# Gate and up products with two moving halves side by side, and identity transposes queued ahead of TensorE's waits, in a two-block transformer kernel

## The chip, the cores and the metric

The kernel runs on one core of a Trainium2 chip. The metric is the time of one execution on the device in microseconds (us), the median of several. TensorE multiplies matrices and writes to eight banks of PSUM, VectorE and ScalarE do the elementwise work, GpSimd takes some of it, and SyncE issues most DMAs. A bank holds 512 float32 values in each of 128 partitions.

## The reference

Two blocks follow each other, all in float32. The change touches the feed-forward layers of the first block, the norm ahead of the feed-forward in both layers of the second block, the very first norm, and the start of the attentions of the first block.

```python
D_MODEL, SEQ, FFN_HIDDEN = 1024, 256, 2816

def rms_norm(x, g):
    return x * rsqrt(mean(x * x, -1) + EPS) * g

def swiglu(h, w_gate, w_up, w_down):
    return (silu(h @ w_gate) * (h @ w_up)) @ w_down

# first block, for each of 2 layers: x is (256, 1024)
x = x + mixer(rms_norm(x, mix_norm))
x = x + memory_cross_attention(rms_norm(x, x_norm), rms_norm(mem, mem_norm), ...)
x = x + swiglu(rms_norm(x, ffn_norm), w_gate, w_up, w_down)

# second block, for each of 2 layers: h is (256, 1024), hc is (256, 1024)
h = h + g1 * mix                     # mix from a modulated norm of h
h = h + g2 * sq_relu_mlp(modulate(rms_norm_2(h, norm2_g), sh2, sc2), w_ff1, w_ff2)
# in layer 0 the same for hc; its 256 tokens stand beside those of h
```

## The kernel before

**Split products.** A float32 product is made of three. Each operand x is held as a high part (rounded to the format fp32r) and a low part (x minus the high part), and a product is high*high + high*low + low*high. Activations lie as [feature, token], eight tiles of 128 features (`KD` = 8) by `S` = 256 tokens. Weights come from memory as pieces of 512 KB, four of which fit in `RAW`. Two pieces make one unit: 1024 rows by 256 columns of a weight matrix. ScalarE rounds a piece to its high part (L1473), VectorE subtracts it from the raw values (L2024, which also frees the piece in `RAW` for the next DMA). Two split units fit (`NSPLIT` = 2), so unit s is split once TensorE has finished with unit s-2, and TensorE waits for the last L2024 of a unit before it starts on it. Below, "the split" of a unit is these four instructions, two on each engine.

**Two ways to order a unit on TensorE.** `project` (L787) keeps one bank for both 128-column halves of a unit and for each half and feature tile issues three matmuls of 256 columns: weights high by activations high (L696), high by low (L697), low by high (L698). `side_by_side` (L722) gives each 128-column half a bank of its own. Its left half collects high*high plus low*high, its right half high*low, so that one matmul of 512 columns takes the activations' high and low parts side by side (L746, the first one L742), and one of 256 columns the low weights (L745, L743). The two halves of the bank have to be added afterwards: ScalarE or VectorE copies or adds the one, VectorE adds the other. Before, the down products of the first block and the feed-forward of layer 1 of the second block use `side_by_side`; the gate and up products use `project`. In layer 1 of the second block ScalarE copies the right half of a bank (L1926), and VectorE adds the left half to it (L2700).

**The four accumulators.** `bank()` hands out PSUM banks `acc0` to `acc3` in turn; TensorE waits until the bank of four groups ago has been read. `pst`, `pso` and `pss` are banks for other uses.

**The feed-forward of the first block.** Its 2816 hidden features go in three chunks of 8, 8 and 6 tiles. A chunk is made in pairs of units, gate and up, four pairs, four and three: 22 units in a layer, 44 in all. The norm's factor for each token is applied to the products: VectorE multiplies the gate bank by it (L2177), ScalarE takes the SiLU (L1810), VectorE multiplies by the factor again (L2544) and by the up bank (L2548), ScalarE rounds the result (L1569), VectorE takes the low part (L2047). The first gate unit is followed by the sums of squares for the norm, and the factor is known only after the first up unit, when `spread` (L882) has copied it to all partitions. Between these stand the splits of later units, in an order written out by hand. In layer 0 GpSimd issues 16 DMAs of 476 KB (`skew`), one for each second split.

**Norms.** `mean_square` (L872) sums squares over the partitions with a matrix of ones, ScalarE takes the root (L1553), VectorE inverts it (L2073), `spread` (L882) copies it to all partitions, and VectorE (L2100, L2145, L2047, L2050) and ScalarE (L1569, L1582) make the normed tiles, one after the other. The product behind a norm takes the feature tiles as they come (`arriving`, L711 to L713, or `side_by_side` with `ready`).

**Attentions.** `attention` (L908) issues for a pair of heads the scores (L921), the transposes of the probabilities (L933) and the sums over values (L948), one pair ahead of the other engines' softmax. The first block has in layer 0 an attention of 16 heads, in layer 1 one of 16, and in each a cross attention of four.

## Time and profile before

| | us |
|---|---|
| median of 3 runs | 2003.89 |
| lowest, highest | 2003.71, 2009.75 |
| the profiled execution, its own time | 2004.48 |
| its span, first to last instruction | 2002.6 |
| TensorE busy | 1940.7 (97%) |
| VectorE, ScalarE busy | 1261.5, 885.9 |

Times in the profile count from the start of the span. The profile lists for each stretch the clock that TensorE was granted: 1.00 is 2.4 GHz and 0.50 is 1.2 GHz. A matmul's own duration includes the time until its result is written, and the next one starts earlier than that, so what a stream of matmuls costs is read from the distance of their starts. The mean granted clock over the span is 0.994.

### The profile page before, as it was taken

The numbers are of one execution on the slowest core, as the hardware profiler recorded it, in microseconds if no ns is written. First come the engines' busy times: TensorE is split into PE (matmuls) and PEld (weight loads), VectorE is DVE, ScalarE is ACT, GpSimd is POOL, SyncE is SP. The second block draws the span as 40 slices with busy tenths as digits, with TensorE's granted clock in tenths as the row PEclk, the third lists the DMA queues.
The fourth block names the chain that finished last, engine by engine and source line by source line (L and its number), as shares of the span: only waits on it lengthen the run. The fifth ranks groups of instructions, "written<-read, shape, count | busy, mean of one in ns | idle before, by whom it ended". The sixth has DMA issues, their size and how long they took to land.

```text
span 2002.6 us, 33109 instructions
## 1 busy us (share of the span) xinstructions
PE 1940.7 (97%) x13572; PEld 1703.3 (85%) x13572; DVE 1261.5 (63%) x2184; ACT 885.9 (44%) x1508; POOL 167.0 (8%) x187
## 2 busy tenths in 40 slices
PE   7999999999999999999999999999999999999998
PEld 7769999998689999978688887888888998997887
DVE  6765666677556666544434447667677745677776
ACT  5655543445565444424532334322232536455443
POOL 0220000002103100002511000000000012000000
PEclk9999999999999999999999999999999999999999
DMA  7365699955646565323533333454656422664554
GB/s 239 102 214 165 157 234 220 220 171 165 224 145 189 182 214 161 116 77 125 163 96 100 95 106 110 133 179 155 197 180 198 139 85 62 186 195 140 182 183 137
DMA packets 313325, 317.56 MB, mean 159 GB/s; under 512 B 17079, under 2 KB 291398, under 8 KB 312918
## 3 DMA queue, kind: packets, MB, share of 16 engines
q1 hardware_dynamic: 308156, 301.65, 49.6%
q0 software_dynamic: 3904, 12.03, 3.0%
q8 instruction: 108, 1.77, 0.4%
q10 hardware_dynamic: 1114, 1.76, 0.3%
q14 instruction: 43, 0.35, 0.1%
HBM read 306.54 MB, written 8.85 MB: 157 GB/s over the span
## 4 chain that ended last, share of the span: by engine, by line
PE 86%; DVE 7%; ACT 3%; DMA 2%; issue 1%; POOL 0%; SPq 0%; DVEq 0%; ACTq 0%; POOLq 0%
PE acc L696 20%; PE acc L697 19%; PE acc L698 19%; PE acc L746 8%; PE acc L745 4%; DVE w_low L2024 3%; PE pss L921 2%; PE acc L742 1%; PE acc L711 1%; ACT w_high L1473 1%; PE pst L933 1%; PE acc L712 1%; PE acc L713 1%; DMA raw<-in_w_mod 1%; PE acc L948 1%
## 5 line engine op out<-in xcount | busy, mean ns | idle before, releaser
L2024 DVE TENSOR_TENSOR w_low<-raw,w_high 128x1024 fp32r<-128x1024 f32 (+4 forms) x503 | 561.1, 1156 | 140.5 <-ACT w_high L1473 137.3
L1473 ACT ACTIVATE w_high<-raw 128x1024 fp32r<-128x1024 f32 (+4 forms) x503 | 471.7, 984 | 375.6 <-PE acc L698 234.2
L696 PE MATMUL acc<-normed,w_high 128*128 128x256 f32 (+1 forms) x1768 | 565.6, 320 | 0.7 <-DVE w_low L2024 0.6
L698 PE MATMUL acc<-normed,w_low 128*128 128x256 f32 (+1 forms) x1768 | 560.6, 317 | 0.0
L697 PE MATMUL acc<-normed,w_high 128*128 128x256 f32 (+1 forms) x1768 | 560.6, 317 | 0.0
L696 PEld LDWEIGHTS acc<-normed,w_high 128*128 128x128 f32 x1768 | 336.1, 190 | 27.0 <-issue 2.0
L698 PEld LDWEIGHTS acc<-normed,w_low 128*128 128x128 f32 x1768 | 336.2, 190 | 22.5
L697 PEld LDWEIGHTS acc<-normed,w_high 128*128 128x128 f32 x1768 | 336.3, 190 | 22.0
L746 PE MATMUL acc<-inner,w_high 128*128 128x512 f32 x612 | 218.2, 396 | 0.0
L696 PE MATMUL acc<-inner,w_high 128*128 128x512 f32 (+2 forms) x576 | 197.3, 343 | 2.2 <-DVE w_low L2024 2.0
L697 PE MATMUL acc<-inner,w_high 128*128 128x512 f32 (+2 forms) x576 | 196.0, 340 | 0.0
L698 PE MATMUL acc<-inner,w_low 128*128 128x512 f32 (+2 forms) x576 | 195.9, 340 | 0.0
L745 PE MATMUL acc<-inner,w_low 128*128 128x256 f32 x612 | 170.7, 279 | 0.0
L746 PEld LDWEIGHTS acc<-inner,w_high 128*128 128x128 f32 x612 | 114.9, 188 | 23.4
L696 PEld LDWEIGHTS acc<-inner,w_high 128*128 128x128 f32 (+1 forms) x576 | 108.4, 188 | 16.6 <-DVE w_low L2024 2.4
L745 PEld LDWEIGHTS acc<-inner,w_low 128*128 128x128 f32 x612 | 115.3, 188 | 4.2
L698 PEld LDWEIGHTS acc<-inner,w_low 128*128 128x128 f32 (+1 forms) x576 | 108.4, 188 | 12.2
L697 PEld LDWEIGHTS acc<-inner,w_high 128*128 128x128 f32 (+1 forms) x576 | 108.5, 188 | 12.1
L1569 ACT ACTIVATE inner<-probs_t 128x512 fp32r<-128x512 f32 x79 | 49.6, 629 | 140.0 <-DVE probs_t L2548 82.0
L696 PE MATMUL acc<-w_high,normed 128*128 128x256 f32 (+1 forms) x336 | 96.9, 289 | 0.6 <-ACT resid L1490 0.6
L697 PE MATMUL acc<-w_low,normed 128*128 128x256 f32 (+1 forms) x336 | 94.9, 282 | 0.0
L698 PE MATMUL acc<-w_high,normed 128*128 128x256 f32 (+1 forms) x336 | 94.9, 282 | 0.0
(281 smaller groups left out, 2685.9 us busy)
## 6 DMA issues: line engine op xcount, KB each, us to landing
raw<-in_w_ff SPq DMA_DIRECT2D x128, 512.0 KB, 4.2
raw<-in_w_mod SPq DMA_DIRECT2D x96, 512.0 KB, 4.4
raw<-in_w_in SPq DMA_DIRECT2D x84, 512.0 KB, 4.1
raw<-in_l_w_gate SPq DMA_DIRECT2D x44, 512.0 KB, 5.5
raw<-in_l_w_up SPq DMA_DIRECT2D x44, 512.0 KB, 4.5
raw<-in_l_w_down SPq DMA_DIRECT2D x32, 512.0 KB, 4.5
raw<-in_l_w_qkv SPq DMA_DIRECT2D x24, 512.0 KB, 4.6
raw<-in_l_w_out SPq DMA_DIRECT2D x16, 512.0 KB, 4.4
```

What stands on the lines that cost most here:

```text
L696: mm(dst, lh, rh, start=i == 0, stop=False)
L697: mm(dst, lh, rl, start=False, stop=False)
L698: ins = mm(dst, ll, rh, start=False, stop=i == n - 1)
L711: mm(dst, lh, rh, start=k == 0 and j == 0, stop=False)
L712: mm(dst, lh, rl, start=False, stop=False)
L713: ins = mm(dst, ll, rh, start=False, stop=k == kt - 1 and j == len(outs) - 1)
L745: mm(b[:, 0:S], wl[:, k, c], high, start=False, stop=False)
L746: ins = mm(out, wh[:, k, c], two, start=False, stop=k == kt - 1)
L921: ins = mm(PSS[e][:, at:at + k.shape[1]], q, k, start=True, stop=True)
L1473: nc.scalar.activation(WH[:, s % NSPLIT, w0:w0 + nw], RAW[:, r:r + nw], ACT.Copy).then_inc(w_high, 1)
L1569: nc.scalar.activation(d.high, tmp_like(i, d.high), ACT.Copy).then_inc(high_done, 1)
L2024: V.tensor_tensor(WL[:, s % NSPLIT, c], RAW[:, r:r + nw], WH[:, s % NSPLIT, c].bitcast(F32), ALU.subtract).then_inc(w_low, 1)
```

## The change

It has four parts.

1. Gate and up products go by `side_by_side`. What `project` put in one bank for a unit now lies in two, in halves to be added. New helpers do that, `second_halves` on ScalarE (into `SM` for the gate, into `TMP` for up) and `first_halves` on VectorE. The multiplication by the norm's factor reads SBUF now.
2. ScalarE and VectorE take the split behind an up unit ahead of rounding the pair's result (`highs`, `flush`); before, it came behind.
3. Three norms get transposes of the identity matrix into a bank that is unused at the time (`keep_busy`): 6 before the input has arrived, 8 ahead of `spread` and 14 behind it in the first norm; in the feed-forward norms of the second block 5 ahead of the last two tiles' squares, 12 and 24 around `spread` in layer 0, 8 and 14 in layer 1.
4. The attentions get them as well: 9 and 7 at the first of layer 0, 5 and 6 at the first of layer 1, 15 at each cross attention.

```diff
+            def keep_busy(n, spare):
+                for _ in range(n):
+                    nc.tensor.transpose(spare[:, 0:P], ident, ident)
...
-            def mean_square(sq, nt, T):
+            def mean_square(sq, nt, T, busy=0):
                 for k in range(nt):
+                    if k == nt - 2:
+                        keep_busy(busy, PSO)
...
                 for j in range(pairs + 2):
+                    keep_busy(busy.get((j, "turn"), 0), PSACC[st["acc"] % 4])
                     if 0 < j <= pairs:
                         turn(2 * j - 2)
                     if j + 1 < pairs:
+                        keep_busy(busy.get((j, "scores"), 0), PSO)
...
+                    keep_busy(busy.get((j, "second"), 0), PSO)
                     if 0 < j <= pairs:
                         turn(2 * j - 1)
...
+            keep_busy(6, PSO)
             pe.wait_ge(x_in, 16)
...
             mean_square(sq_x, KD, S)
+            keep_busy(8, PSO)
             spread(S)
+            keep_busy(14, PSO)
...
-                attention(x_tasks, ...)
+                attention(x_tasks, ..., busy={(2, "turn"): 15})
...
-                        project(1, at_pair, ready=ready)
+                        side_by_side(1, at_pair, ready=ready)
                         mean_square(sq1, KD, S)
-                        project(1, at_pair)
+                        side_by_side(1, at_pair)
                         spread(S)
-                        project(tiles - 2, at_pair)
+                        side_by_side(tiles - 2, at_pair)
...
-                mean_square(sq2 if T == 2 * S else sq1, KD, T)
+                mean_square(sq2 if T == 2 * S else sq1, KD, T, busy=5)
+                keep_busy(12 if T == 2 * S else 8, PSO)
                 spread(T)
+                keep_busy(24 if T == 2 * S else 14, PSO)
...
+            def second_halves(dst):                        # ScalarE
+                for j in range(2):
+                    b, free = bank()
+                    nc.scalar.activation(dst[:, S * j:S * j + S], b[:, S:2 * S], ACT.Copy).then_inc(relu_done, 1)
...
+            def first_halves(dst):                         # VectorE
+                for j in range(2):
+                    b, free = bank()
+                    st["relu"] += 1
+                    dve.wait_ge(relu_done, st["relu"])
+                    half = dst[:, S * j:S * j + S]
+                    V.tensor_tensor(half, half, b[:, 0:S], ALU.add).then_inc(free, 1)
+                    own(free)
```

**TensorE, one tile of a gate unit.** In the rows of an order, `acc<-normed,w_high` is the output bank and what is read, and the sizes are columns of the output. Before:

```order
L696 MATMUL acc<-normed,w_high 128x256
L697 MATMUL acc<-normed,w_high 128x256
L698 MATMUL acc<-normed,w_low 128x256
L696 MATMUL acc<-normed,w_high 128x256
L697 MATMUL acc<-normed,w_high 128x256
```

and after (L746 and L747 are the lines L745 and L746 of before):

```order
L747 MATMUL acc<-normed,w_high 128x512
L746 MATMUL acc<-normed,w_low 128x256
L747 MATMUL acc<-normed,w_high 128x512
L746 MATMUL acc<-normed,w_low 128x256
```

Three matmuls of 256 columns have become one of 512 and one of 256.

**VectorE, one pair in the middle of a chunk.** `scores` is the tile `SM`, `probs_t` the tile `TMP`, `inner` the pair's result. Before:

```order
L2177 SCALAR_TENSOR_TENSOR scores<-acc,scores 128x512
L2024 TENSOR_TENSOR w_low<-raw,w_high 128x1024 x2
L2544 TENSOR_TENSOR scores<-scores 128x512
L2548 TENSOR_TENSOR probs_t<-scores,acc 128x512
L2047 TENSOR_TENSOR inner<-probs_t,inner 128x512
```

and after:

```order
L2319 TENSOR_TENSOR scores<-scores,acc 128x256 x2
L2570 TENSOR_TENSOR scores<-scores 128x512
L2043 TENSOR_TENSOR w_low<-raw,w_high 128x1024 x2
L2573 TENSOR_TENSOR scores<-scores 128x512
L2319 TENSOR_TENSOR probs_t<-probs_t,acc 128x256 x2
L2578 TENSOR_TENSOR probs_t<-scores,probs_t 128x512
L2043 TENSOR_TENSOR w_low<-raw,w_high 128x1024 x2
```

Four additions are new, and the second split (the last row) has moved ahead of the low part of the result, which follows it.

**TensorE, the feed-forward norm of layer 0 in the second block.** `work` holds the squares, `cst` the constants. Before:

```order
L872 MATMUL acc1<-work,cst 32x128 x32
L882 MATMUL pst<-rstd,cst 128x128 x4
L711 MATMUL acc2<-normed,w_high 128x512
L712 MATMUL acc2<-normed,w_high 128x512
L713 MATMUL acc2<-normed,w_low 128x512
```

and after:

```order
L875 MATMUL acc1<-work,cst 32x128 x24
L897 MATMUL pso<-cst 128x128 x5
L875 MATMUL acc1<-work,cst 32x128 x8
L897 MATMUL pso<-cst 128x128 x12
L885 MATMUL pst<-rstd,cst 128x128 x4
L897 MATMUL pso<-cst 128x128 x24
L712 MATMUL acc2<-normed,w_high 128x512
```

41 transposes (L897) stand in the queue ahead of the waits for the last squares, for the inverse root and for the first normed tile.

## Rows read from the trace of the kernel before

**Rows 1.** The page: which engine holds the chain that ended last.
```profile
PE 86%; DVE 7%; ACT 3%; DMA 2%; issue 1%; POOL 0%; SPq 0%; DVEq 0%; ACTq 0%; POOLq 0%
```

**Rows 2.** TensorE in four stretches: stretch, length, busy (records), clock, DMA share, GB/s.
```profile
628.20:708.87 80.67, 80.67 (x674) 1.00 0.59 181
232.94:314.30 81.36, 81.13 (x675) 1.00 0.95 223
708.87:731.25 22.38, 22.38 (x130) 1.00 0.66 201
1878.28:1901.50 23.22, 22.83 (x130) 1.00 0.52 163
```

**Rows 3.** TensorE in a down unit, in order of time: start, duration, line, operands.
```profile
710.32 0.28 PE L745 MATMUL acc<-inner,w_low 128*128 128x256 f32 x1
710.44 0.40 PE L746 MATMUL acc<-inner,w_high 128*128 128x512 f32 x1
710.67 0.28 PE L745 MATMUL acc<-inner,w_low 128*128 128x256 f32 x1
```

**Rows 4.** Groups by line, 636 to 706 and 1878.2 to 1901.4: count, busy, mean ns, idle before.
```profile
L1473 ACT ACTIVATE w_high<-raw 128x1024 fp32r<-128x1024 f32 x25 | 25.0, 1047 | 14.7 <-PE acc L698 14.7
...
L2024 DVE TENSOR_TENSOR w_low<-raw,w_high 128x1024 fp32r<-128x1024 f32 x26 | 30.7, 1222 | 4.1 <-ACT w_high L1473 4.1
...
L2700 DVE TENSOR_TENSOR scores<-scores,acc 128x256 f32<-128x256 f32 x7 | 2.9, 417 | 2.5 <-ACT scores L1926 2.4
...
L1926 ACT ACTIVATE scores<-acc 128x256 f32<-128x256 f32 x8 | 3.0, 376 | 6.9 <-PE acc L746 6.9
```

**Rows 5.** Weight pieces, from issue to landing, in 243 to 314 (layer 0), then 636 to 706 (layer 1).
```profile
DMA to landing us min/median/max: 3.6/7.3/10.6
...
DMA to landing us min/median/max: 3.5/4.4/5.5
```

**Rows 6.** VectorE in order of time in the first pair of layer 0.
```profile
237.25 1.23 DVE L2024 TENSOR_TENSOR w_low<-raw,w_high 128x1024 fp32r<-128x1024 f32 x1 [1.80 <-ACT w_high L1473]
239.20 0.69 DVE L2544 TENSOR_TENSOR scores<-scores 128x512 f32<-128x512 f32 x1 [0.72 <-ACT scores L1810]
```

**Rows 7.** Half-clock stretches: length, busy of PE, PEld, DVE, ACT, POOL, then clock.
```profile
17.00:20.30 3.30, 3.28 (x15) 2.84 (x14) 3.23 (x8) 1.65 (x3) 0.00 (x0) 0.50 1.05 415
...
597.30:600.60 3.30, 3.05 (x10) 2.09 (x8) 1.72 (x2) 0.22 (x1) 0.00 (x0) 0.50 0.44 105
...
1208.30:1211.60 3.30, 3.30 (x9) 2.55 (x9) 3.23 (x9) 1.82 (x4) 0.00 (x0) 0.50 0.00 0
...
1805.60:1812.30 6.70, 6.05 (x18) 4.89 (x19) 6.41 (x15) 3.09 (x7) 0.00 (x0) 0.50 0.01 2
```

**Rows 8.** TensorE's transposes of the inputs, first at the start, then at 24 us.
```profile
6.26 3.65 PE L1075 MATMUL acc<-cst,work 128*128 128x128 f32 x16 [6.26 <-DMA work<-in_x]
...
24.01 1.91 PE L1075 MATMUL acc<-cst,work 128*128 128x128 f32 x16
```

**Rows 9.** TensorE in the cross attention and at its output product, layer 0, then layer 1.
```profile
201.61 0.63 PE L933 MATMUL pst<-cst,scores 128*128 128x128 f32 x4 [2.02 <-DVE scores L2380]
...
207.42 0.47 PE L711 MATMUL acc<-inner,w_high 128*128 128x256 f32 x1
...
595.39 0.63 PE L933 MATMUL pst<-cst,scores 128*128 128x128 f32 x4 [2.02 <-DVE scores L2380]
...
602.68 0.47 PE L711 MATMUL acc<-inner,w_high 128*128 128x256 f32 x1
```

**Rows 10.** The chain of waits behind the feed-forward norm of layer 0, second block.
```profile
1218.91 2.28 DVE w_low L2024 x2
1221.24 0.50 PE acc L696
```

**Rows 11.** Layer 1: TensorE's L742 (ns min/median/max, first and last start), VectorE's split.
```profile
L742 PE MATMUL acc<-normed,w_high x3: 398/628/765, 1806.2 to 1814.9; 128*128 128x512 f32 x3
...
1811.78 2.35 DVE L2024 TENSOR_TENSOR w_low<-raw,w_high 128x1024 fp32r<-128x1024 f32 x2
```

More of the change, by code:

```diff
@@ L558, in build @@
         gated = sem("gated")
+        gate_scaled = sem("gate_scaled")
         rot_done = sem("rot_done")
@@ L906, in rotate, with attention @@
                     ins.then_inc(acc_full, 1)
-            def attention(tasks, mods=0, lead=None, tail=None, keys=None, ropes=None, late=None):
+            def attention(tasks, mods=0, lead=None, tail=None, keys=None, ropes=None, late=None, busy={}):
                 first, pairs = st["task"], len(tasks) // 2
@@ L1159, in _ @@
                     attention(swa_tasks + mla_tasks, MODS, lead=mla_lead, tail=heads_product, late=SWA_H // 2,
-                              keys=st["acc"] - 3)
+                              keys=st["acc"] - 3, busy={(1, "scores"): 9, (2, "turn"): 7})
                 else:
@@ L1175, in _ @@
                     values(1)
-                    attention(dil_tasks, MODS, lead=lambda: values(1), tail=heads_product)
+                    attention(dil_tasks, MODS, lead=lambda: values(1), tail=heads_product, busy={(1, "scores"): 5, (1, "second"): 6})
                 pe.wait_ge(cols_free, st["pair"])
@@ L1184, in _ @@
                 project(2, at_pair, ready=by_tile(S))
-                attention(x_tasks, lead=lambda: values(1, blocks=(2, 3)), keys=st["acc"] - 2)
+                attention(x_tasks, lead=lambda: values(1, blocks=(2, 3)), keys=st["acc"] - 2, busy={(2, "turn"): 15})
                 project(2, ot, m=4, kt=4, ready=by_head_tile(4))
@@ L1923, in _ @@
                             if l:
-                                for j in range(2):
-                                    b, free = bank()
-                                    nc.scalar.activation(SM[:, st["sig"] % 2, S * j:S * j + S], b[:, S:2 * S],
-                                                         ACT.Copy).then_inc(relu_done, 1)
+                                second_halves(SM[:, st["sig"] % 2, :])
                                 st["sig"] += 1
@@ L2540, in _ @@
                                 rooted_row()
-                            times_row(gate, g)
+                            V.tensor_tensor(gate, gate, RROW2, ALU.mult).then_inc(gate_scaled, 1)
                             split()
@@ L2544, in _ @@
                             link(V.tensor_tensor(gate, gate, RROW2, ALU.mult))
-                            b, free = bank()
                             i = room()
                             d = hidden(c, S).tiles(m, m + 2)
-                            V.tensor_tensor(TMP[:, i % 2, :].rearrange("p (a n) -> p a n", a=2), gate,
-                                            b[:].rearrange("p (a n) -> p a n", a=2), ALU.mult).then_inc(free, 1)
+                            up = TMP[:, i % 2, :]
+                            first_halves(up)
+                            V.tensor_tensor(up, raw_gate, up, ALU.mult).then_inc(val_done, 1)
                             pending.append((i, d, None))
-                            flush()
                             if m or c:
                                 split()
+                            flush()
                     else:
@@ L2694, in _ @@
                                 st["sig"] += 1
-                                for j in range(2):
-                                    b, free = bank()
-                                    st["relu"] += 1
-                                    dve.wait_ge(relu_done, st["relu"])
-                                    half = s[:, S * j:S * j + S]
-                                    V.tensor_tensor(half, half, b[:, 0:S], ALU.add).then_inc(free, 1)
-                                    own(free)
+                                first_halves(s)
                                 V.scalar_tensor_tensor(TMP[:, i % 2, :], s, 0.0, s, ALU.max, ALU.mult)\
```

22 lines of the change are left out of this document (11 added, 11 removed).

## The prediction

> **What bounds the kernel now.** First I read who holds the chain that ended last: TensorE for 86% of it, VectorE 7% [rows 1]. So an edit counts by what it does to the distance between TensorE's matmuls and to its waits. Then I read windows. Fourteen gate and up units take 80.67 us in layer 1 of the first block with no idle time, so a unit costs 80.67/14 = 5.762 us, and its 48 matmuls of 256 columns 0.120 us each. In layer 0 the same fourteen take 81.36 us, 5.811 each: 0.7 us more, at a DMA share of 0.95 against 0.59 [rows 2]. Third, the four places at half the clock that the change aims at [rows 7].
>
> **Part 1, the products.** Four down units, already in the new form, take 22.38 us, 5.595 each, with nothing idle [rows 2]. There the 256 columns cost 710.44 - 710.32 = 0.12 us and the 512 columns 710.67 - 710.44 = 0.23 [rows 3], where three of 256 cost 0.36. A unit saves 5.762 - 5.595 = 0.167 us. There are 44, 22 in each layer: **7.4 us** if TensorE stays the bound, 3.7 in each layer.
>
> The Trainium skill, page "TensorE: Matmul & The Clock Gate", section "Back-to-back issue gap", gives a single warm matmul as its columns divided by 2.4 GHz plus 2.5 ns, which makes the merger worth 2.5 ns. By that the 704 mergers would save 1.8 us. The rows above show about 10 ns for each, and they decide.
>
> What is added is on the other engines. For each pair ScalarE gets four copies of 0.376 us and VectorE four additions of 0.417 [rows 4]. VectorE then has in a pair of 2 x 5.595 = 11.19 us: four L2024 of 1.222 = 4.9, four additions = 1.7, four operations of 512 columns of 0.69 (L2544's duration [rows 6]) = 2.8, together 9.3. ScalarE has four L1473 of 1.047, four copies and two more operations, of 0.7 at most each, about 7.1 [rows 4]. Neither is the bound, so what matters is the order. After a gate unit ends come one copy 0.38, two additions 0.83, the factor 0.69, the split's two L2024 2.44: 4.3 us, and TensorE needs that split 5.6 us after. After the up unit: 0.38 + 0.83 + 0.69 (product) + 2.44 = 4.3, again of 5.6. So the slack is 1.3 us, thanks to part 2, which puts the split ahead of the pair's result. The low part of the result (0.69) comes after, at 5.0, before the next gate unit ends at 5.6. What hides the copies and additions is thus 1.3 us; each us beyond it in a unit is paid in full.
>
> Every product now waits in two banks of the ring of four. In the middle of a chunk the banks come free as said, 1.2 us after their unit ends, and are wanted at 5.6: no wait. The first pair of layer 0 is the exception. VectorE's L2024 for the second piece of a late unit runs from 237.25 to 238.48, and it multiplies by the factor (L2544) at 239.20 to 239.89 [rows 6]. The new addition for the first up unit stands behind that and frees its first bank at 239.9 + 0.4 = 240.3. The second up unit wants that bank when the second gate unit ends: 232.94 [rows 2] less 0.3 (two faster units) plus 5.6 = 238.2. A new wait of **2.1 us**, bounded by 0 (if the pieces land earlier) and 3.5 (if the factor and the SiLU slip as far again as an L2024). In layer 1 I expect none: the DMA share is 0.59.
>
> The DMAs: four pieces fit, each is wanted once in a pair, and a landing plus L1473 and L2024 (1.05 + 1.22) has to fit in 11.2 us: it may take 8.9, before it was 11.5 - 2.3 = 9.2. In layer 1 landings take 4.4 us median, 5.5 at most: no matter. In layer 0 the median is 7.3, the longest 10.6 [rows 5]: some are over either bound, and TensorE's 0.7 us of waits there come from them. Each late one now costs up to 0.3 more. With all eleven pairs that is 3.7, with none it is 0, and the wait in the first pair may even absorb the 0.7 of before. I take **0.4**, near the low end, since the median is under the bound.
>
> Products: 3.7 + 3.7 - 2.1 - 0.4 = **4.9 us**, between 0 and 8.1.
>
> **Parts 3 and 4, the transposes.** A transpose costs 0.109 us at the full clock ((1.91 - 0.27)/15 between starts) and 0.215 at half ((3.65 - 0.42)/15) [rows 8]. TensorE did nothing but such transposes from 6.26 us on, and the full clock was there at 10.1, so transposes raise it. Whether five to fifteen of them also keep it from falling, no row shows: bounds nothing and all.
>
> The same page, section "Part 4: PE-mode transpose", says that "HAM K=8/8 doesn't engage for transpose-mode", which would make this half of the change worth nothing. The start of this trace speaks against it; the time that it would give is rival B.
>
> The queues ahead of the attentions' waits: 15 at the cross attention are 1.64 us in a wait of 2.02 and what follows it [rows 9]; those at the heads (9, 7, 5, 6) are 0.98 us at most in waits of like length. I charge nothing for them; if a wait is shorter than its transposes, the rest is paid, 0.3 us at most each. In order of time:
>
> - The six before the input land in idle time, but the last may overrun: -0.1.
> - 16.95 to 20.36, first norm: half the clock under 3.28 us of busy TensorE, so at most 1.6. But the tiles that it multiplies come from VectorE, busy for 3.23 of the 3.30 us [rows 7]; were it alone the bound, the gain would be 0. I take 0.6, nearer to that.
> - 597.2 to 600.6, the cross attention of layer 1. From the first transposes to the output product layer 0 takes 207.42 - 201.61 = 5.81 us, layer 1 602.68 - 595.39 = 7.29 [rows 9], and the latter holds a stretch at half the clock [rows 7]. At the full clock 7.29 becomes 5.81: +1.5, the best founded of them. In layer 0 there is nothing to gain.
> - 1208.2 to 1211.6, the norm of layer 0 in the second block. VectorE makes the tiles, again busy for 3.23 of 3.30 us [rows 7], and the unit behind waits for VectorE's L2024, 1218.91 + 2.28, TensorE starting at 1221.24 [rows 10]: what TensorE gains before that it waits there. No gain. Five transposes ahead of the last squares (0.55 us) partly delay the chain: -0.3.
> - 1805.5 to 1812.4, layer 1. Half the clock costs 6.05/2 = 3.0 us of work [rows 7], but the unit behind needs the low weights, ready at 1811.78 + 2.35 = 1814.1, and starts at 1814.9 [rows 11]. It can come no earlier than 1814.1: +0.8.
>
> Transposes: -0.1 + 0.6 + 1.5 - 0.3 + 0.8 = **2.5 us**, between -0.7 (none works, each place overruns) and 4.5.
>
> **The sum.** 4.9 + 2.5 = 7.4 us. The profiled execution took 2004.48, so it would take 1997.1; the median is 0.6 lower, so I predict **1996.5 us**.
>
> **Rivals.**
>
> A, the forecast: 1996.5. Chance 0.45.
>
> B, transposes do not hold the clock. For: nowhere in the trace does a short run of them stand in a wait. Against: the clock at 10.1 us. Then products 4.9 less 0.4 of overruns: 2003.9 - 4.5 = 1999.4. Chance 0.13.
>
> C, the chain through banks and splits bounds the units. For: in layer 1 of the second block four such units, with the same copies, additions and a result rounded ahead of the split, take 23.22 us, 5.805 each, TensorE idle for 0.4 of it [rows 2]. Against: there the rounding stood ahead of the split, and part 2 takes that out. If it holds, 44 units at 5.805 against 22 at 5.762 and 22 at 5.811 lose 0.8, and with the first pair's part of the wait some 1.8; the clock gives its 2.5: 2003.9 + 1.8 - 2.5 = 2003.2. Chance 0.20.
>
> D, all works: no wait at the first pair, no late pieces, the 0.7 us of layer 0 gone: 8.0, and the clock 4.2 (norm tiles come as fast as TensorE takes them): 1991.7. Chance 0.17.
>
> E, slower. Layer 0's pieces run against GpSimd's DMAs. If a faster TensorE frees `RAW` so that all pieces land like the slowest of today, 10.6 us [rows 5], a pair takes 10.6 + 2.3 = 12.9 where it took 11.5 with its own slack: 1.4 x 11 = 15.4 us in that layer, less layer 1's 3.7 and the clock's 2.5: 2003.9 + 15.4 - 6.2 = 2013. It decides from a median landing of 9.2 us on. Against: the median is 7.3, and the bytes are the same. Chance 0.05.
>
> **How the numbers follow.** What a measurement of this kernel can tell from no change is about 0.3%, 6.0 us: faster means under 1997.9. A lies 1.4 us under it, and its own spread (the bounds of the first pair and of the late pieces) reaches over it in a quarter of A's cases, so 0.34 of A and D's 0.17 are faster, and 0.04 of B, if its overruns cost nothing and the first pair is cheap: 0.55. The rest of A and B, and C: 0.40 within. E: 0.05. The range, from 1991.5 (D) to 2003.5 (C), leaves out E and the outer sides of D and C, together some 0.2.
>
> **What would show it.** Right: fourteen gate and up units of layer 1 in 78.3 us with nothing idle; a wait of about 2 us for a bank before the second up unit of layer 0; the granted clock at 1.00 at 597, 1208 and 1806; 5.8 us from the transposes to the output product in both layers; the second unit at 1814 still waiting for the low weights. Wrong: units at 5.8 us with TensorE released by L2024 (C), stretches at 0.50 in their old places (B), landings over 9 us in layer 0 (E), no wait in the first pair (D).

## The result, and the profile after

The changed kernel takes 1995.09 us, the median of four executions (1994.43 to 1997.97). The kernel before took 2005.11 beside it (median of four, 2003.71 to 2009.75). The ratio is 0.995, with a 95% interval of 0.9937 to 0.9963: 10 us faster, between 7 and 13. The forecast was 1996.5 us and 7.4 us faster. One execution of the kernel before (3192.75 us) and one of e1 (2392.15 us), with granted clocks of 0.557 and 0.749, are left out of the ranges and ratios below.

The page of after, its busy times and the chain that ended last, to be set beside [rows 1]:

```profile
PE 1946.0 (98%) x13021; PEld 1675.6 (84%) x13021; DVE 1291.2 (65%) x2272; ACT 913.6 (46%) x1596; POOL 168.9 (8%) x187
...
PE 86%; DVE 7%; ACT 3%; DMA 1%; issue 1%; POOL 0%; ACTq 0%; DVEq 0%; POOLq 0%
```

TensorE still is the bound. VectorE and ScalarE have 30 and 28 us more work than before, and their shares of the chain are the same.

The windows of after, the columns as in [rows 7]: twelve gate and up units of layer 1, ten of layer 0, then the four places that had the lower clock:

```profile
633.03:700.16 67.13, 67.13 (x386) 58.49 (x386) 53.15 (x74) 38.19 (x60) 14.48 (x13) 1.00 0.62 195
257.87:313.80 55.93, 55.93 (x321) 48.73 (x320) 43.70 (x60) 31.75 (x50) 4.54 (x5) 1.00 0.91 232
...
593.20:596.60 3.40, 2.71 (x15) 2.18 (x14) 1.74 (x3) 1.43 (x4) 0.00 (x0) 1.00 0.70 197
1198.00:1201.40 3.40, 3.10 (x15) 2.13 (x13) 3.33 (x9) 1.55 (x4) 0.00 (x0) 1.00 0.00 0
1796.00:1803.00 7.00, 5.75 (x32) 4.24 (x31) 6.52 (x16) 3.50 (x8) 0.00 (x0) 1.00 0.00 0
17.00:20.30 3.30, 2.54 (x17) 2.15 (x18) 3.23 (x8) 1.26 (x2) 0.00 (x0) 1.00 1.04 416
```

A unit takes 67.13/12 = 5.594 us in layer 1 and 55.93/10 = 5.593 in layer 0, TensorE busy throughout: the 5.595 of the down units of [rows 2], to the last digit but one. The granted clock is 1.00 at all four places.

The first pair of layer 0, in order of time (before: [rows 6]):

```profile
235.97 1.06 ACT L1489 ACTIVATE w_high<-raw 128x1024 fp32r<-128x1024 f32 x1 [2.60 <-DMA raw<-in_l_w_up]
237.05 1.28 ACT L1833 ACT_TABLE_LOAD   x1
237.06 1.23 DVE L2043 TENSOR_TENSOR w_low<-raw,w_high 128x1024 fp32r<-128x1024 f32 x1 [1.62 <-ACT w_high L1489]
...
239.01 0.69 DVE L2573 TENSOR_TENSOR scores<-scores 128x512 f32<-128x512 f32 x1 [0.72 <-ACT scores L1833]
239.73 0.88 DVE L2319 TENSOR_TENSOR probs_t<-probs_t,acc 128x256 f32<-128x256 f32 x2
240.30 0.47 PE L743 MATMUL acc<-normed,w_high 128*128 128x512 f32 x1 [1.56 <-DVE probs_t L2319]
```

This is the wait that the forecast named: a late piece (ScalarE waited 2.60 us for it), then the SiLU, the factor, and the addition L2319 that frees the bank. TensorE is released by it at 240.30, where the forecast had 240.3.

**Where the time went, place by place.** The same instruction can be found in two traces; the difference of its starts says how far the one is ahead there. The table gives what each stretch gained over the profiled execution of before (minus: lost). The stretches are told by the times of before. The columns are the changed kernel, a second trace of it, and five of the experiments below.

| stretch (before) | forecast | after | again | e1 | e2 | e3 | e10 | e11 |
|---|---|---|---|---|---|---|---|---|
| start to 24 | +0.5 | -0.14 | -0.30 | +0.30 | -1.34 | -0.02 | +0.32 | +0.77 |
| 24 to 225 | 0 | +0.19 | -1.95 | -0.37 | +0.01 | -2.23 | -1.35 | +0.06 |
| 225 to 418, layer 0's feed-forward | +1.2 | +2.61 | +1.53 | +1.23 | +0.97 | -4.11 | +4.66 | +5.17 |
| 490 to 526, modulation products | 0 | +2.16 | +0.72 | +1.14 | +2.49 | +1.74 | +1.16 | +1.01 |
| 590 to 601, cross attention | +1.5 | +1.48 | +1.48 | +0.26 | +1.48 | +1.48 | +1.48 | +1.48 |
| 620 to 766, layer 1's feed-forward | +3.7 | +3.26 | +3.36 | +3.37 | 0.00 | -0.77 | +3.32 | +3.37 |
| 766 to 1195 | 0 | +0.01 | -1.57 | +0.05 | -1.58 | -0.03 | +0.04 | -0.36 |
| 1195 to 1254, norm | -0.3 | -0.55 | -0.57 | -0.14 | -0.57 | -0.56 | -0.57 | +0.02 |
| 1795 to 1866, norm | +0.8 | +0.68 | +0.68 | +0.52 | +0.69 | +0.71 | +0.68 | +0.72 |
| whole span | +7.4 | +9.96 | +3.59 | +6.58 | +2.24 | -3.60 | +9.95 | +12.39 |

Some rows hardly differ between executions of one order of work (the cross attention, the two norms, layer 1's feed-forward). Five rows do, by one to three microseconds: the start, 24 to 225, layer 0's feed-forward, 490 to 526, and 766 to 1195. Some of that is stretches of 3.4 us at the lower clock that come in one trace and not in the next, as at 242 us in e1's, inside layer 0's feed-forward. Medians, not one trace, say what those rows are worth.

### The profile page after: what moved, and what is told of

It reads as the page before. It is cut to its first block, busy times and chain, and to the rows that moved or that the text cites. A ratio compares the mean times of both kernels' runs of the same rounds, so it can differ in the third digit from the quotient of the medians.

```text
span 1992.6 us, 32294 instructions
## 1 busy us (share of the span) xinstructions
PE 1946.0 (98%) x13021; PEld 1675.6 (84%) x13021; DVE 1291.2 (65%) x2272; ACT 913.6 (46%) x1596; POOL 168.9 (8%) x187
## 4 chain that ended last, share of the span: by engine, by line
PE 86%; DVE 7%; ACT 3%; DMA 1%; issue 1%; POOL 0%; ACTq 0%; DVEq 0%; POOLq 0%
PE acc L697 16%; PE acc L699 16%; PE acc L698 16%; PE acc L747 15%; PE acc L746 7%; DVE w_low L2043 3%; PE acc L743 2%; PE pss L929 2%; PE pst L941 1%; ACT w_high L1489 1%; PE acc L712 1%; PE acc L744 1%; PE acc L819 1%; PE acc L956 1%; PE acc L713 1%
## 5 line engine op out<-in xcount | busy, mean ns | idle before, releaser
L2043 DVE TENSOR_TENSOR w_low<-raw,w_high 128x1024 fp32r<-128x1024 f32 (+4 forms) x503 | 560.6, 1155 | 125.1 <-ACT w_high L1489 122.8
L1489 ACT ACTIVATE w_high<-raw 128x1024 fp32r<-128x1024 f32 (+4 forms) x503 | 471.6, 985 | 329.9 <-PE acc L699 181.8
L697 PE MATMUL acc<-normed,w_high 128*128 128x512 f32 (+2 forms) x1096 | 375.0, 342 | 0.4 <-DVE w_low L2043 0.3
L699 PE MATMUL acc<-normed,w_low 128*128 128x512 f32 (+2 forms) x1096 | 370.6, 338 | 0.0
L698 PE MATMUL acc<-normed,w_high 128*128 128x512 f32 (+2 forms) x1096 | 370.5, 338 | 0.0
L747 PE MATMUL acc<-normed,w_high 128*128 128x512 f32 x840 | 299.2, 396 | 0.0
L746 PE MATMUL acc<-normed,w_low 128*128 128x256 f32 x840 | 234.7, 279 | 1.1 <-DVE normed L2069 1.0
L697 PEld LDWEIGHTS acc<-normed,w_high 128*128 128x128 f32 (+1 forms) x1096 | 207.6, 189 | 26.0 <-issue 2.0
L699 PEld LDWEIGHTS acc<-normed,w_low 128*128 128x128 f32 (+1 forms) x1096 | 207.6, 189 | 22.3
L698 PEld LDWEIGHTS acc<-normed,w_high 128*128 128x128 f32 (+1 forms) x1096 | 207.7, 189 | 22.1
L747 PE MATMUL acc<-inner,w_high 128*128 128x512 f32 x612 | 218.2, 396 | 0.0
L747 PEld LDWEIGHTS acc<-normed,w_high 128*128 128x128 f32 x840 | 157.7, 188 | 32.3
L746 PE MATMUL acc<-inner,w_low 128*128 128x256 f32 x612 | 170.8, 279 | 0.0
L746 PEld LDWEIGHTS acc<-normed,w_low 128*128 128x128 f32 x840 | 158.3, 188 | 7.3 <-DVE normed L2069 2.0
L747 PEld LDWEIGHTS acc<-inner,w_high 128*128 128x128 f32 x612 | 114.9, 188 | 23.3
L746 PEld LDWEIGHTS acc<-inner,w_low 128*128 128x128 f32 x612 | 115.3, 188 | 4.2
```

Of the source, the lines that this page charges most:

```text
L697: mm(dst, lh, rh, start=i == 0, stop=False)
L698: mm(dst, lh, rl, start=False, stop=False)
L699: ins = mm(dst, ll, rh, start=False, stop=i == n - 1)
L746: mm(b[:, 0:S], wl[:, k, c], high, start=False, stop=False)
L747: ins = mm(out, wh[:, k, c], two, start=False, stop=k == kt - 1)
L1489: nc.scalar.activation(WH[:, s % NSPLIT, w0:w0 + nw], RAW[:, r:r + nw], ACT.Copy).then_inc(w_high, 1)
```

## The experiments

Each was run beside the kernel before; a ratio has its 95% interval with it. The kernel before had medians of 2006.94 beside e1 to e4, 2008.12 beside e5 to e8, 2005.48 beside e9 to e11 and 2009.24 beside e12, so kernels of different groups are compared by ratio.

### e1: the products alone

```diff
             def keep_busy(n, spare):
-                for _ in range(n):
+                for _ in range(0):
```

> The changed kernel without any transposes of the identity: parts 1 and 2 alone. Theory 1 (the terms add up): the two feed-forwards of the first block end 6.2 us earlier than before, as they do with everything in (2.8 in layer 0, 3.4 in layer 1), and the low clock is back in its four places; time 6 us under the kernel before, ratio 0.997. Theory 2 (the faster products only pay because the clock no longer falls near them): under 4 us. If the 2.6 us that the changed kernel gained in the modulation's products at 500 to 526 us come with the faster products, the time is 8 to 9 us under the kernel before, and that stretch is again short of waits; if they are chance, the waits there are anything between those of the two traces.

2001.74 us (1997.74 to 2006.19), ratio 0.9972 (0.9962 to 0.9982): 5.6 us faster, where theory 1 had 6 and the forecast's products 4.9. The low clock is back in all four places, and came in two others (105 and 242 us). Three of these windows:

```profile
16.40:19.80 3.40, 3.40 (x16) 3.25 (x17) 3.33 (x9) 1.26 (x2) 0.00 (x0) 0.50 1.03 412
593.20:596.60 3.40, 3.31 (x10) 2.47 (x10) 2.94 (x5) 1.48 (x4) 0.00 (x0) 0.50 0.00 0
1200.90:1207.50 6.60, 5.80 (x14) 4.58 (x15) 6.46 (x17) 3.27 (x8) 0.00 (x0) 0.50 0.00 0
```

### e2: the transposes alone

The kernel before with `keep_busy` and all its calls, and nothing else of the diff.

> The kernel before with all the transposes of the identity and nothing else of the change: parts 3 and 4 alone. Theory 1: the granted clock is 1.00 from 10 us to the end, layer 1's cross attention gives 1.5 us, the norm of layer 1 in the second block 0.8, the first norm 0.5 (less what a late constant costs), the norm at 1208 us costs 0.3: 2.5 us under the kernel before, ratio 0.9988. Rival: transposes do not hold the clock, and the four stretches are back: 0 to 0.6 us slower than before. Rival 2: the modulation's waits at 500 to 526 us go away with them, then 5 us under.

2002.9 us (2000.21 to 2008.08), ratio 0.9981 (0.9972 to 0.9989): 3.8 us faster, where 2.5 were expected. By the interval it is 2.2 to 5.6, which holds the 2.5 as well. The two halves, 5.6 and 3.8, add up to 9.4 of the 10 us. Why it may be more than 2.5 the executions' mean granted clocks suggest. The eleven with transposes had 0.997 to 0.999; the 28 of the kernel before that ran beside them had 0.990 to 0.995, the median 0.992. The one profiled execution of before, on which the forecast rests, had 0.994: less time at the lower clock than most of these. Among the 28, the eleven at 0.991 or less have a median time of 2007.4 us and the seven at 0.993 or more one of 2005.9. That has the right sign and size, but at every clock the executions scatter by some microseconds, so the explanation is argued and not shown. Rival 2, that the waits at 500 to 526 us go with the transposes, the traces refute (see e7). In the trace of e2 the clock is 1.00 from 14.4 us to 1994 but for 3.4 us at 854.

### e3: the changed kernel with part 2 undone

```diff
+                            highs([hidden(c, S).tiles(m, m + 2)])
                             if m or c:
                                 split()
-                            highs([hidden(c, S).tiles(m, m + 2)])
...
+                            flush()
                             if m or c:
                                 split()
-                            flush()
```

> The changed kernel with part 2 undone: in a pair the rounding of the result and its low part stand ahead of the split behind the up unit again. My working gave the chain behind an up unit 4.3 us of 5.6; with the product's rounding (0.6) and its low part (0.69) ahead of the split it has 5.6 to 5.8. Theory 1: TensorE waits 0 to 0.25 us for the split in each pair, 22 pairs: 0 to 5 us slower than the changed kernel, I expect 3 (ratio to the kernel before 0.9965). Rival (the slack was larger than worked out, because the two engines overlap): no difference, 0.995.

2009.07 us, ratio 1.0011 (1.0002 to 1.002): **slower than the kernel before**, and 0.6% (12 us) slower than the changed kernel by the two ratios. I had expected 3 and at most 5. A window of four units in the middle of layer 1's feed-forward:

```profile
677.44:700.70 23.26, 22.92 (x130) 19.50 (x129) 17.81 (x24) 12.73 (x20) 3.72 (x4) 1.00 0.60 185
```

23.26/4 = 5.815 a unit, close to the 5.805 of the last of [rows 2]: rival C's mechanism. In order of time, in one pair:

```profile
667.00 0.69 DVE L2578 TENSOR_TENSOR probs_t<-scores,probs_t 128x512 f32<-128x512 f32 x1
667.72 0.63 ACT L1591 ACTIVATE inner<-probs_t 128x512 fp32r<-128x512 f32 x1 [1.31 <-DVE probs_t L2578]
668.26 1.99 ACT L1489 ACTIVATE w_high<-raw 128x1024 fp32r<-128x1024 f32 x2
668.38 0.69 DVE L2066 TENSOR_TENSOR inner<-probs_t,inner 128x512 fp32r<-128x512 f32 x1 [0.70 <-ACT inner L1591]
669.34 2.36 DVE L2043 TENSOR_TENSOR w_low<-raw,w_high 128x1024 fp32r<-128x1024 f32 x2 [0.26 <-ACT w_high L1489]
...
671.75 0.50 PE L743 MATMUL acc<-normed,w_high 128*128 128x512 f32 x1 [0.17 <-DVE w_low L2043]
```

The split's L1489 starts only after the result's rounding, and then L2043 has to wait for it: 0.70 + 0.26 us in which VectorE does nothing. I had added up durations on one engine, 5.6 to 5.8 us, and left out these two handovers. With the split first, L1489 runs beside the product and L2043 follows without a wait, as in the changed kernel:

```profile
655.89 2.00 ACT L1489 ACTIVATE w_high<-raw 128x1024 fp32r<-128x1024 f32 x2
656.12 0.42 DVE L2319 TENSOR_TENSOR probs_t<-probs_t,acc 128x256 f32<-128x256 f32 x1 [1.12 <-ACT probs_t L1512]
656.58 0.69 DVE L2578 TENSOR_TENSOR probs_t<-scores,probs_t 128x512 f32<-128x512 f32 x1
657.19 2.35 DVE L2043 TENSOR_TENSOR w_low<-raw,w_high 128x1024 fp32r<-128x1024 f32 x2
```

In layer 0 the loss is larger. What ended TensorE's idle time from 205 to 421 us (us, times), in e3 and then in the changed kernel:

```profile
  DVE w_low L2043: 4.6, 13
  DVE probs_t L2319: 1.2, 1
```

```profile
  DVE probs_t L2319: 1.6, 1
...
  DVE w_low L2043: 0.6, 2
```

Thirteen waits for a split instead of two. Part 2 alone, on the kernel before, was not run. There TensorE was busy for all of the 80.67 us in layer 1 [rows 2], and in the trace it waited for splits for 1.3 us in all from 205 to 421 us, so the order alone had little to give.

### e4: the up unit's additions earlier in the first pair

```diff
                             if m == c == 0:
                                 root(KD, S)
                                 split()
+                                act.wait_ge(stored, st["store"] - 1)
+                                second_halves(TMP[:, st["store"] % 2, :])
                             split()
...
-                            act.wait_ge(stored, st["store"] - 1)
-                            second_halves(TMP[:, st["store"] % 2, :])
                             if m or c:
+                                act.wait_ge(stored, st["store"] - 1)
+                                second_halves(TMP[:, st["store"] % 2, :])
                                 split()
...
                             V.tensor_tensor(gate, gate, RROW2, ALU.mult).then_inc(gate_scaled, 1)
+                            if m == c == 0:
+                                i = room()
+                                up = TMP[:, i % 2, :]
+                                first_halves(up)
                             split()
...
-                            first_halves(up)
+                            if m or c:
+                                i = room()
+                                up = TMP[:, i % 2, :]
+                                first_halves(up)
```

> The changed kernel, but in the first pair of each layer the copies and additions for the up unit stand ahead of the second split instead of behind the SiLU. Theory 1: the wait of 1.8 us ahead of layer 0's second up unit is one for the up unit's bank alone; it goes, 1.5 us are gained, and TensorE next waits for the late piece's low weights, if at all. Rival: the second up unit would be held by the late weight piece just as long (its L2043 ended at 238.3, TensorE was ready at 238.5), then 1.5 us show up later, at the next late piece: no gain in the total.

1996.89 us, ratio 0.995 (0.9937 to 0.9963), the changed kernel's own. In the trace the wait at 240 is gone and another of 0.95 us stands ahead of the unit at 248.0; layer 0's feed-forward gains 3.9 us over before, layer 1's 3.0, 0.3 less than without the edit. So in this trace it moves a wait and keeps part of what it saves; in the time nothing of it shows.

### e5 and e6: six and five transposes fewer

e5 leaves out `keep_busy(6, PSO)` ahead of the input, e6 the `busy=5` of the norms' sums of squares.

> The changed kernel without the six transposes ahead of the input. In all four traces with them TensorE waited 0.7 to 0.85 us for a part of the constants at 10.6 to 10.7 us, in the two without them it started on these at 9.8 and 9.9. Theory 1 (the six delay that part, or what is issued around it): the wait is gone, and the second batch of input transposes starts 0.5 to 0.8 us earlier than in the changed kernel, at 23.4 to 23.7. Rival (it is chance): the wait is there again. Of the clock: it was full from 9.6 to 10.1 without the six and at 9.1, 9.9, 14.4 and 14.4 with them; if the six decide it, it is full by 10.2 here.

1997.97 us, ratio 0.9943 (0.9929 to 0.9958). TensorE did not wait for the constants (10.07), but e8, also without the six, waited 0.62 us until 10.70, and the constants' DMA landed at 10.66 there: theory 1 falls. The full clock came at 11.8 us here, later than the 10.2 expected; with the six it came anywhere from 8.2 (e11) to 14.4 us (e2, e4), and e12, without any transposes, lost it again at 14.8. So neither hangs on the six.

> The changed kernel without the five transposes ahead of the last two tiles' squares in the two norms of the second block. They put TensorE 0.8 us behind at 1201 and at 1801, of which the trace of the changed kernel had 0.25 left at 1254 and nothing at 1802. Theory 1: without them the squares come 0.8 us earlier, the clock stays at 1.00 by the transposes around the spreading alone, and 0.3 to 0.6 us are gained at 1208. Rival: the clock falls to 0.50 in one or both stretches, as before, and 0.8 us are lost in layer 1.

1996.98 us, ratio 0.994 (0.9923 to 0.9956). The norm at 1195 to 1254 gains 0.03 us over before, where every trace with the five loses 0.55 to 0.57, and the clock stays at 1.00 there and at 1800: theory 1, 0.6 us. (In layer 1 the five cost nothing: the norm at 1795 to 1866 gains about 0.7 with them and without.) The profiled execution itself was one of 2005.26, with a long low stretch (44.7 to 54.9 us) and a landing of 11.6 us, and layer 0's feed-forward is 2.1 us slower in it than before; its three others took 1996.05 to 1997.12.

### e7: the changed kernel again

> The changed kernel once more, for a second trace of it. If its gain of 2.6 us at 500 to 526 us is a property of the kernel, the waits for the modulation's weights there are again about 2.6 us shorter than in the trace of before; if they are chance, this differs by about a microsecond. Same question for stretches at the lower clock in odd places (84 and 86 us in two experiments, 105 and 242 in a third, 854 in a fourth, none in the first trace of the changed kernel).

2000.58 us, ratio 0.9957 (0.9942 to 0.9971). The column "again" of the table. TensorE's waits for the modulation's weights between 494 and 527 us, by start, in before, then after, then e7:

```profile
501.91 0.64 PE L818 MATMUL acc<-raw,silc 128*32 128x256 f32 x8 [0.30 <-DMA raw<-in_w_mod]
...
514.47 0.64 PE L818 MATMUL acc<-raw,silc 128*32 128x256 f32 x8 [0.92 <-DMA raw<-in_w_mod]
...
526.02 0.64 PE L818 MATMUL acc<-raw,silc 128*32 128x256 f32 x8 [1.18 <-DMA raw<-in_w_mod]
```

```profile
499.75 0.64 PE L819 MATMUL acc<-raw,silc 128*32 128x256 f32 x8 [0.79 <-DMA raw<-in_w_mod]
```

```profile
503.17 0.64 PE L819 MATMUL acc<-raw,silc 128*32 128x256 f32 x8 [0.83 <-DMA raw<-in_w_mod]
...
521.85 0.64 PE L819 MATMUL acc<-raw,silc 128*32 128x256 f32 x8 [0.39 <-DMA raw<-in_w_mod]
...
526.03 0.64 PE L819 MATMUL acc<-raw,silc 128*32 128x256 f32 x8 [0.76 <-DMA raw<-in_w_mod]
```

The stretch gained 2.16 us in the first trace of the changed kernel and 0.72 in the second; e2, whose products are the old ones, gained 2.49. Of the traces that have the transposes, e4's lost 0.4 there and e8's gained 0.2; e12's, which has neither the products nor the transposes, gained 1.6. It belongs to no edit. Twelve of the thirteen other traces gain there, so the profiled execution of before was an unlucky one at this place. The same holds the other way at 84.6 and 852.6 us, where e7 had 3.4 us at the lower clock each and the first trace none.

### e8: ScalarE's SiLU ahead of the late piece

e4 without the six transposes, and in layer 0's first pair the SiLU stands ahead of the second split.

> The kernel with the early additions in the first pair, without the six transposes at the start, and in layer 0 with ScalarE's SiLU of the first pair ahead of the second split. Theory 1: TensorE's wait at 248 us (1.2 us in the kernel with the early additions alone) came from the first pair's chain, SiLU to addition to the next gate bank, and shrinks to 0.3 to 0.6; with the start it takes 1993.5 to 1994.5 where the changed kernel takes 1995.1. Rival: the wait at 248 is one for a late weight piece, then it stays, or 0.3 to 0.5 come on top, since the high parts of the late unit are now taken later.

1998.24 us, ratio 0.995 (0.9935 to 0.9965): no gain. The wait moved to the unit at 245.3 (0.64 us), and one of 0.96 came at 274.9. The wait lies between what the two theories expected (0.3 to 0.6, and 1.2 or more), and the time that theory 1 gave did not come.

### e9: transposes at 81 us

```diff
                     def mla_lead():
+                        keep_busy(14, PSO)
                         wh, wl = w = grid(take(2, 1024), 2, 1024)
...
-                mean_square(sq2 if T == 2 * S else sq1, KD, T, busy=5)
+                mean_square(sq2 if T == 2 * S else sq1, KD, T)
```

> The changed kernel with 14 more transposes in TensorE's wait of 1.98 us at 81 us (ahead of the latent heads' product), and without the five ahead of the last squares. In five of the seven traces with transposes so far that followed the changed kernel's order the clock was at 0.50 for 3.4 us from 83.5 to 89 us, which costs 1.4 us. Theory 1: transposes in the wait hold the clock, no low stretch there, mean granted clock 0.998 to 0.999 in every execution, and with the five gone (0.6 us) the kernel is 1.5 to 2 us faster than the changed kernel in the median. Rival: low stretches at 84 us come from something else and are there as often; 0.6 us.

1996.71 us, ratio 0.9959 (0.9946 to 0.9971): no gain to be seen. TensorE at the wait, and a window behind it, in e7 and then in e9:

```profile
83.49 0.39 PE L697 MATMUL acc<-inner,w_high 128*128 128x256 f32 x1 [1.98 <-DVE w_low L2043]
...
84.60:88.00 3.40, 3.40 (x18) 3.40 (x18) 3.11 (x8) 3.39 (x12) 0.48 (x1) 0.51 0.85 251
```

```profile
81.45 1.75 PE L897 MATMUL pso<-cst 128*128 128x128 f32 x14
83.49 0.39 PE L697 MATMUL acc<-inner,w_high 128*128 128x256 f32 x1 [0.30 <-DVE w_low L2044]
...
84.60:88.00 3.40, 3.40 (x30) 3.40 (x30) 3.10 (x8) 3.39 (x12) 0.49 (x1) 1.00 0.82 240
```

TensorE gets through 30 matmuls in the 3.4 us instead of 18, and both traces with the 14 transposes (e9, e11) have the full clock. But the wait was followed by a full clock in six of the twelve traces without them as well (before, after, e1, e2, e8, e12), and e9's six executions have the mean clocks of the others (0.997 to 0.999). Two traces are too few: whether the transposes help at this place stays open.

### e10: GpSimd's DMAs in halves

```diff
-                for i in range(16):
-                    pool.wait_ge(w_low, split_pieces[ffn_split[0] + 2 * i - 1])
-                    l, j = i // 8, i % 8
-                    src = bass.AP(..., ap=[[6400, 120], [0, 8], [1, 127]])
-                    pool.dma_start(SKEW[l][:, 8 * j:8 * j + 8, :], src).then_inc(skew_w, 16)
+                for i in range(32):
+                    pool.wait_ge(w_low, split_pieces[ffn_split[0] + i - 1])
+                    l, j = i // 16, i % 16
+                    src = bass.AP(..., ap=[[6400, 120], [0, 4], [1, 127]])
+                    pool.dma_start(SKEW[l][:, 4 * j:4 * j + 4, :], src).then_inc(skew_w, 16)
...
```

> The changed kernel with GpSimd's 16 DMAs of 476 KB in layer 0 cut in 32 of 238 KB, one for each split instead of one for each second. Theory 1 (TensorE's late weights in layer 0 are the pieces that are issued together with one of these DMAs): the longest landing falls from 9.4 to 9.6 us to about 8, the late piece of the first pair comes 1 us earlier, and layer 0's feed-forward gains 1 to 2 us: its gain over the kernel before was 1.5, 2.6 and 1.3 us in three traces, where layer 1's is 3.3. Rival (late landings come from the total of the bytes, or elsewhere): no difference.

1994.26 us (1991.37 to 1995.11), ratio 0.9946 (0.9933 to 0.9959), not to be told from the changed kernel's 0.995. What follows stands in the traces. The weight pieces from issue to landing, 225 to 314 us, in after and then in e10:

```profile
DMA to landing us min/median/max: 3.5/6.0/9.6
```

```profile
DMA to landing us min/median/max: 3.8/6.2/7.8
```

The median stays, the tail goes, and not in this pair alone. The longest landing of this stretch is 9.2 to 11.6 us in all eleven traces with the whole DMAs, and 7.8 to 8.4 in the three with the halves (e10 to e12). In each of the eleven it is that of a piece issued 0.3 us ahead of one of GpSimd's DMAs.

What ended TensorE's idle time from 205 to 421 us, in e10 (to be set beside the rows of e3 above):

```profile
  ACT probs_t L1640: 0.7, 1
  DVE w_low L2043: 0.4, 2
```

TensorE no longer waits for L2319, and the order of the first pair is unchanged; in the seven traces with this wait it was 1.1 to 2.9 us long. e4 removes it too, with the whole DMAs, by moving the additions. So the wait takes both, the late piece and the additions that stand behind it, and either edit removes it. Layer 0's feed-forward gains 4.66 us here. With the changed kernel's order there and the whole DMAs it gains 2.61, 1.53, 1.23, 1.25 and 2.09 (after, e7, e1, e5, e9) and loses 2.1 in e6's execution of 2005.26 us; e1 and e5 have a stretch of 3.4 us at the lower clock in it. e4 gains 3.9. So e10's gain is the largest of these, and e11's 5.17 is larger still, but with a trace each and a spread of 1.4 us and more between traces of one order, its size is not settled.

### e11: all of it together

e9 and e10, and e4's edit in layer 0 alone.

> Everything that looked useful: the transposes at 81 us in and the five ahead of the squares out, the halved DMAs, and the early additions in layer 0's first pair alone (in layer 1 they cost 0.3 us). If the gains add up, 1.5 to 2 for the first, 1 to 2 for the second and 1 for the third: 3 to 5 us under the changed kernel in the same call, ratio to the kernel before 0.9925 to 0.9935. Rival: the early additions and the halved DMAs remove the same wait, then 2.5 to 3.5 us.

1993.16 us (1991.46 to 1996.12), ratio 0.9946 (0.9932 to 0.996). The gains do not add up: e10 alone has the same ratio. In the same group e9 took 1996.71 and e10 1994.26. In its trace layer 0's feed-forward gains 5.17 us, the most of all. Its median is the lowest of all the kernels here, but its interval overlaps the changed kernel's and e10's, so I call it no better than either.

### e12: the halved DMAs on the kernel before

> The kernel before with GpSimd's DMAs in layer 0 halved as in e10, nothing else. There TensorE waited 0.3 us at the first pair and 0.6 at 320, and 0.9 to 1.1 us for pieces in all. Theory 1 (the late pieces cost the new products more than the old ones, because a pair is shorter and its chain longer): layer 0's feed-forward ends 0.7 to 1.5 us earlier than before, where the same edit gave the changed kernel 2.0 to 3.1 us in the traces; ratio 0.9993 or so, not to be told from no change. Rival (the halves help both alike): 2 to 3 us, ratio 0.9987.

2004.23 us, ratio 0.9979 (0.9967 to 0.9991). The median says 4.2 us, nearer to the rival than to theory 1; the trace says 1.6 for layer 0's feed-forward, where e2, with the old products and the whole DMAs, has 0.97: a difference within what this stretch varies by. By the ratio the old products gain from the halves too (1.8 to 6.6 us), while between the changed kernel and e10 it shows no gain. Whether the new products gain more is not settled, nor what the halves are worth to them.

## Why the prediction was right, point by point

**The products.** The term of 7.4 us was worked out as 44 x 0.167 with a unit of 5.595; the units take 5.593 and 5.594. Layer 1 gave 3.26 to 3.38 of its 3.7 in every trace with the changed kernel's order; what the last 0.3 went into is not traced. The Trainium skill, page "TensorE: Matmul & The Clock Gate", section "Back-to-back issue gap", would give 2.5 ns for a merger, 1.8 us in all; e1 alone shows 5.6 (3.6 or more by its interval), so the measured distances decide.

**The slack and part 2.** The forecast gave the chains 4.3 us of 5.6, and TensorE waits for no split in a steady pair: right. What the text did not see is how much hangs on part 2. The step said that it is "thanks to part 2", and rival C had its price: units of 5.805. e3 has 5.815, and 12 us. C had the right price of a unit, and of layer 1 (0.9 us lost, e3's trace 0.77), for the kernel without part 2. In layer 0 it was too cheap: 0.9 us with its part of the first pair, where e3's trace lost 4.11. For the kernel with part 2, no unit of the windows shows C's wait.

**The first pair and the late pieces.** The wait was forecast at 2.1 us, released by the addition at 240.3; it was 1.7 (the unit's last matmul starts at 238.34, and the next could have started 0.23 later) and in e7 2.2 us. The cause was named only in half. The bank is held since a piece lands 9.6 us after its issue, 0.3 us after which GpSimd's DMA was issued; in e10, with these in halves, it lands after 7.6 and the bank is free in time. The gain of 1.2 us for layer 0 was too low against 2.61 in the first trace and near 1.53 in the second and 1.23 in e1: within the spread of this stretch. So the 0.4 us for late pieces is neither confirmed nor refuted.

**The clock.** The cross attention of layer 1 was forecast at 1.5 and gave 1.48 in every trace with transposes, 0.26 in e1's without. The norm at 1806 gave 0.68 of 0.8 (e1, without transposes and with the low clock there, has 0.52, and e12, without any of the four parts, 0.3, so less than I credited is the clock's). The norm at 1208 lost 0.55 where 0.3 was forecast; e6, e9 and e11 show that it is the five transposes. The start lost 0.14 instead of gaining 0.5: the product behind the norm did gain 0.5 by the full clock, and a constant came 0.85 us late.

The weak step here is another: I took the low stretches of one profiled execution for those of the kernel. That execution had a mean clock of 0.994; the medians of before beside the experiments were 0.992, 0.991, 0.994 and 0.992. The transposes measured 3.8 us and not 2.5, but the interval (2.2 to 5.6) holds both, so this error is likely and not shown.

The rule of the Trainium skill (same page, "Part 4: PE-mode transpose") that a transpose does not count for the clock would have given rival B; e2, where transposes are the only change, has 0.998 against 0.992, so these transposes contradict it. (The profile lists them as matmuls and does not say in which mode they ran.)

**Why the gain came out 2.6 us larger.** In the profiled pair 2.16 us come from the waits at 490 to 526, which no edit caused. In the medians e1 has 0.7 us more than its part of the forecast and e2 1.3 more, both inside their intervals, so no run shows which term was too small. That the time came within 1.4 us of the median is in part luck. The forecast set out from a median of 2003.89 us, and the kernel before had 2005.11 beside the result, which took 1.2 off the error of 2.6. Single executions say less still: the whole span gained 9.96 us in one trace of the changed kernel and 3.59 in the next.

**The rivals.** B is out by e2. D (all works) did not come: the first pair's wait is there in both traces of the changed kernel. Without that wait, in e10 and e11, the times are 1994.3 and 1993.2 where D had 1991.7. E did not come: landings have medians of 6.0 and 6.9 us in layer 0, not 9.2. (Single landings over 9 us, which the forecast took as E's sign, are there with 9.6 and 10.1, but before had one of 10.6.) C's mechanism is that of e3.

## What to carry to other kernels

Before a product is made cheaper on the bounding engine, write down for each handover between the helping engines when it starts and which engine is idle meanwhile; the order of two steps there was worth more (12 us) than the new products with the right order gain (5.6 us). A wait for a buffer at the end of a long chain may be a late transfer at its start: look at the longest landing, not the median, and at what large DMA is issued just beside it. Before low-clock stretches are priced from one trace, compare its mean clock with those of other executions, since a single trace shows only one draw of them.

## What was not expected of the hardware

- Transposes of the identity alone in TensorE's waits kept the granted clock at 0.997 to 0.999 in 11 executions of e2, where 28 of the kernel before had 0.990 to 0.995 and 11 of e1 0.988 to 0.994.
- Stretches of 3.4 us at 0.50 come in some executions and not in others at the same place: behind the wait of 1.98 us at 81 us in e3, e4, e5, e6, e7 and e10, not in before, after, e1, e2, e8 and e12, nor in e9 and e11 with transposes in the wait.
- A 512 KB piece issued 0.3 us ahead of a DMA of 476 KB from another queue took up to 9.2 to 11.6 us to land in eleven traces, with DMAs of 238 KB up to 7.8 to 8.4 in three. The medians of all pieces were 6.0 to 8.0 and 6.1 to 6.2.
- The first full clock came between 8.2 and 11.8 us in twelve traces and only at 14.4 in two (e2, e4), which were 1.3 to 1.4 us behind at 24 us.
